# Writing the expert loop of the tensor engine's program out straight

## The chip, the core and the metric

One NeuronCore of a Trainium2 chip runs the whole step. The metric is the device time of one execution in microseconds (us); lower is better. Engines are named as in the profile: PE is the tensor engine (PEld its weight loads), DVE the vector engine, ACT the scalar engine, POOL GpSimd, SP the engine that issues nearly all of the transfers.

## The reference, cut to what matters

One layer of a hybrid decoder for 272 prompt and 8 sample rows (the 16 meta rows need no expert work, so 264 rows go on), all in float32. First a mixer (a Mamba-2 group and a convolution group), which the change does not touch. Then a mixture of experts:

```
logits = u @ w_router + b_router            # 32 experts, the top 4 of each row
gt  = min(x @ w_gate[e] + b_gate[e], 7)
up  = clip(x @ w_up[e] + b_up[e], -7, 7)
hdn = (up + 1) * gt * sigmoid(1.702 * gt)
y   = hdn @ w_down[e] + b_down[e]           # times the gate, added into the row
```

Each expert has three 1024 x 1024 float32 matrices, 12 MB, and all 32 experts are read from HBM: 192 pieces of 2 MB. How many rows an expert gets depends on the data and is known only on the chip.

## The kernel before, in words

The experts are sorted on the chip by their number of rows and paired: a round is one big expert (up to 128 rows) and one small expert (up to 32 rows). There are 16 rounds. The weights go through a ring in SBUF of six slots of 2 MB, `landed[0]` to `landed[5]` being the semaphores that tell of their landing: slots 0 and 1 hold w_gate, 2 and 3 w_up, 4 and 5 w_down. SP refills a slot with the next expert's weights as soon as PE tells that it has read it (lines 359 to 367, semaphores `gate_half`, `gate_used`, `piece_used`). So at most six transfers, one expert, are ahead of PE.

A big expert with 64 rows or fewer is narrow: every weight piece is read by PE once (`by_width(count, ...)` takes `what(1)`). One with more is wide: every piece is read twice, once for each half of its rows (`what(2)`). `by_width` (line 1546) builds both variants, so both stand in the program and the one that is not needed is jumped over. The order of PE in a round is: `big_expert` (line 1678): bias, gate pieces with the results of the former expert scattered between them, up pieces, inputs of the small expert gathered, hidden rows turned, down pieces; then `small_expert` (line 1712): gate pieces, with the scatter of the big expert between them (its shape goes by the big expert's width, `former`), up pieces, inputs of the next big expert gathered (its shape goes by `following`), turn, down pieces.

Products of a big expert are recorded at line 1482, of a small one at line 1525, bias products at 1472 and 1515, scatters at 1534 and 1492, gathers at 1503 and 1459, turns at 1228. The first bias of a round is the first group of line 1472 in it, so this line marks where rounds begin. One product in the source is two weight loads and two matmuls in the trace (16 source calls are a row "x32"); a turn is one of each.

Experts 0 and 1 (round 0) are written out ahead of the loop (lines 1738 and 1739). The other 15 rounds are one loop on PE (line 1740). Waits in it compare a semaphore with a register that is computed from the loop's counter, and the two widths that a round needs are read from the list `cnts` in SBUF (`count_of`, line 1553). ACT, DVE and SP run loops of their own, which stay.

Of the kernel before, what the change touches and what calls it, by code (L numbers as in the profile page):

```python
# [24 lines left out]
NE, TOPK = 32, 4  # L25
# [22 lines left out]
def build(nc, I, O):  # L48
    ctx = ExitStack()
    with ctx:  # L50
# [1172 lines left out]
        def _(pe):  # L1223
# [246 lines left out]
            def bias(bank, row):  # L1470
                for h_, dst in enumerate(halves(bank)):
                    MM(dst, oh[row:row + NE, :], brow[row:row + NE, 512 * h_:512 * (h_ + 1)],  # L1472
                       start=True, stop=False, skip_group_check=True)

            def piece_products(p, b, src, bank, fresh, i16):
                pe.wait_ge(landed[p // 2], i16)
                hs = []
                for k in range(2):
                    kk = 2 * (p % 4) + k
                    o = 512 * b + P * (kk % 4) + HALF * (kk // 4)  # L1480
                    for h_, dst in enumerate(halves(bank + b)):
                        hs.append(MM(dst, src[:, o:o + HALF], piece(p)[:, k, 512 * h_:512 * (h_ + 1)],  # L1482
                                     start=(fresh and kk == 0), stop=(kk == KT - 1), skip_group_check=True))
                return hs
# [44 lines left out]
            def scatter_s(m, n4, release=False):  # L1529
                if m:  # L1530
                    pe.wait_ge(ev["acc_done"], n4 + m)
                for h_ in range(2):
                    q = m // 2 + 2 * h_
                    h = MM(ps[:, 6 + h_, 0:TN], ys[QUAR * q:QUAR * (q + 1), P * (m % 2):P * (m % 2 + 1)],  # L1534
                           Pm[QUAR * q:QUAR * (q + 1), 0, :], start=True, stop=True)
                    if release and h_ == 0:
                        h.then_inc(ev["gate_used"], 1)
                h.then_inc(ev["sc_done"], 1)
# [14 lines left out]
            def count_of(i):  # L1553

                return pe.value_load(cnts[0:1, bass.ds(i, 1)], min_val=0, max_val=TN)
# [54 lines left out]
            def up_of(n, i16):  # L1610
                if n == 1:
                    for p in range(4, 8):
                        hs = piece_products(p, 0, xT, 2, False, i16)
                        hs[-1].then_inc(ev["up_first" if p == 7 else "piece_used"], 1)
                else:
                    bias(1, 64)
                    bias(3, 96)
                    for p in range(4):
                        hs = piece_products(p, 1, xT, 0, False, i16)
                        if p % 2:  # L1620
                            hs[-1].then_inc(ev[("gate_half", "gate_used")[p // 2]], 1)
                    for p in range(4, 8):
                        hs = piece_products(p, 0, xT, 2, False, i16)
                    hs[-1].then_inc(ev["up_first"], 1)
                    for p in range(4, 8):
                        hs = piece_products(p, 1, xT, 2, False, i16)
                        if p < 7:
                            hs[-1].then_inc(ev["piece_used"], 1)
# [45 lines left out]
            def former_ready(i):  # L1674
                pe.wait_ge(ev["p_ready"], i + 1)
                pe.wait_ge(ev["y_back"], i * 2 + 64)

            def big_expert(i, count, then=None):
                pe.wait_ge(ev["oh_ready"], i + 1)
                bias(0, 64)  # L1680
                if then:
                    then()
                pe.wait_ge(ev["xt_ready"], i * 2 + 2)
                bias(2, 96)

                def gate_up(n):
                    for p in range(4):
                        hs = piece_products(p, 0, xT, 0, False, i * 16 + 16)
                        if n == 1 and p == 1:
                            hs[-1].then_inc(ev["gate_half"], 1)  # L1690
                        if p == 3:
                            hs[-1].then_inc(ev["gate_done"], 1)
                        if p == (1 if then else 0):
                            former_ready(i)
                        for m in (() if then and p == 0 else (p - 1,) if then and p < 3 else (2, 3) if then else (p,)):
                            scatter_s(m, i * 4, n == 1 and m == 3)
                    if then:
                        pe.wait_ge(ev["order_ready"], 1)
                    up_of(n, i * 16 + 16)

                by_width(count, gate_up)
                pe.wait_ge(ev["s_ready"], i + 2)
                gather_s()
                by_width(count, lambda n: turn_hidden(n, i * 2))
                pe.wait_ge(ev["acc_done"], i * 4 + 4)
                pick_slots()
                pe.wait_ge(ev["xg_out"], i * 2 + 4)
                turn_s(xg, 2, ev["xt_done"])
                by_width(count, lambda n: down_of(n, i * 2, i * 16 + 16))
                pe.wait_ge(ev["ht_ready"], i * 2 + 2)  # L1710

            def small_expert(i, former, following):
                pe.wait_ge(ev["oh_ready"], i + 1)
                pe.wait_ge(ev["xt_ready"], i * 2 + 2)

                def former_rows(n, p):
                    if p == 0:
                        former_ready(i)
                    scatter(n, p, i * 4)

                by_width(former, lambda n: gate_s(i * 16 + 16, lambda p: former_rows(n, p)))
                up_s(i * 16 + 16)
                pe.wait_ge(ev["s_ready"], i + 2)
                by_width(following, gather)
                pe.wait_ge(ev["hdn_ready"], i * 2 + 2)
                turn_s(hdn, 0, ev["ht_done"])
                pe.wait_ge(ev["acc_done"], i * 4 + 4)
                pick_slots()

                def turn_following(n):  # L1730
                    for b in range(n):
                        pe.wait_ge(ev["xg_out"], i * 2 + 3 + b)
                    turn(n, xg, 2, ev["xt_done"])

                by_width(following, turn_following)
                down_s(i * 2, i * 16 + 16)

            big_expert(0, first, find_order)
            small_expert(1, first, count_of(3))
            with pe.Fori(0, NE // 2 - 1) as ii:  # L1740
                count, following = count_of(ii * 2 + 3), count_of(ii * 2 + 5)
                big_expert(ii * 2 + 2, count)
                small_expert(ii * 2 + 3, count, following)
            pe.wait_ge(ev["o_tab"], 1)
            n_over = pe.value_load(otab[0:1, OVER:OVER + 1], min_val=0, max_val=OVER)
            pe.wait_ge(ev["xt_ready"], NE * 2 + 2)
# [103 lines left out]
```

## Time and profile before

| | us |
|---|---|
| three runs | 1265.29, 1269.01, 1271.62 |
| median | 1269.01 |
| the profiled execution's own time | 1267.89 |
| its span, first to last instruction | 1266.1 |
| PE busy in the span | 1171.0 (92%) |
| DVE busy | 487.8 (39%) |
| mean granted PE clock | 0.974 of full speed |

Busy time of PE is modelled at its end and says little by itself. The mixer and the routing take the span up to about 300 us; experts run from there to about 1254 us; the rest is the final norm.

### The profile page before, as it was taken

How to read it: one execution, taken by the hardware profiler on the slowest of the kernel's cores; microseconds unless marked ns; L12 is line 12 of the kernel's file. 1: busy time of each engine (PE TensorE's matmuls, PEld its weight loads, DVE VectorE, ACT ScalarE, POOL GpSimd, SP SyncE). 2: the span in 40 equal slices, each digit the busy share in tenths (PEclk: the TensorE clock that was granted, in tenths of full speed). 3: DMA queues.
4: the chain of work that ended last, by engine and by line, in shares of the span. 5: the costliest groups of instructions: out<-in, count | busy, mean ns of one | idle time of the engine just before them, and what ended most of it. 6: DMA issues, size and time to landing. Idle time of an engine off the chain costs nothing.

```text
span 1266.1 us, 21176 instructions
## 1 busy us (share of the span) xinstructions
PE 1171.0 (92%) x8462; PEld 553.0 (44%) x8463; DVE 487.8 (39%) x1083; ACT 196.0 (15%) x432; POOL 5.4 (0%) x33
## 2 busy tenths in 40 slices
PE   8999989999899999999899999899999888979896
PEld 6888768874333333433333433333433333233233
DVE  2999997015332322232312233222232232323233
ACT  2144513021111111011101111100111111011012
POOL 0000000000000000000000000000000000000000
PEclk9999998999998999999989999999999899999898
DMA  9542338615999999899999999998999999999995
GB/s 394 226 170 88 121 148 313 272 44 193 396 428 424 429 427 424 338 430 429 429 428 386 358 430 429 429 429 353 396 430 429 429 429 427 430 429 428 428 431 215
DMA packets 36996, 451.35 MB, mean 357 GB/s; under 512 B 5112, under 2 KB 5656, under 8 KB 10080
## 3 DMA queue, kind: packets, MB, share of 16 engines
q1 hardware_dynamic: 35344, 449.02, 85.2%
q10 hardware_dynamic: 1616, 1.82, 0.4%
q8 instruction: 26, 0.43, 0.1%
q14 instruction: 10, 0.08, 0.0%
HBM read 443.57 MB, written 7.25 MB: 356 GB/s over the span
## 4 chain that ended last, share of the span: by engine, by line
PE 57%; DMA 28%; DVE 11%; issue 2%; DVEq 1%; ACT 0%; POOL 0%; SPq 0%; POOLq 0%; ACTq 0%
DMA ring<-in_w_experts 28%; PE ps L1482 23%; PE ps L1525 10%; DVE acts L734 5%; PE ps L1254 3%; PE ps L1459 3%; PE ps L1361 3%; PE ps L1418 2%; PE ps L1492 2%; PE ps L1534 2%; PE ps L1228 2%; PE ps L1472 1%; DVE acts L829 1%; PE ps L1352 1%; PE ps L1515 1%
## 5 line engine op out<-in xcount | busy, mean ns | idle before, releaser
L1482 PE MATMUL ps<-ring,extra 128*64 128x512 f32 x1824 | 418.4, 603 | 12.2 <-DMA ring<-in_w_experts 12.2
L1087 DVE TENSOR_TENSOR acts<-ps,acts 128x528 f32<-128x528 f32 x128 | 90.6, 708 | 393.1 <-PE ps L1492 199.5
L1525 PE MATMUL ps<-ring,extra 128*32 128x256 f32 x3072 | 207.2, 405 | 37.0 <-DMA ring<-in_w_experts 31.2
L1482 PEld LDWEIGHTS ps<-ring,extra 128*64 128x64 f32 x1824 | 123.0, 138 | 262.4 <-issue 233.5
L1525 PEld LDWEIGHTS ps<-ring,extra 128*32 128x32 f32 x3072 | 91.2, 114 | 142.6 <-issue 51.4
L734 DVE SCALAR_TENSOR_TENSOR acts<-acts,small 128x256 f32<-128x256 f32 x224 | 91.2, 474 | 1.1 <-ACT acts L461 1.1
L1254 PE MATMUL ps<-acts,ring 128*128 128x280 f32 (+1 forms) x320 | 75.3, 394 | 0.3 <-ACT ring L534 0.3
L1254 PEld LDWEIGHTS ps<-acts,ring 128*128 128x128 f32 x320 | 60.5, 190 | 14.2 <-issue 1.0
L1254 PE MATMUL ps<-acts,extra 128*128 128x280 f32 x256 | 61.3, 400 | 1.9 <-DVE acts L716 1.9
L1101 DVE TENSOR_SCALAR extra<-ps 128x512 f32<-128x512 f32 x32 | 22.0, 689 | 97.6 <-PE ps L1482 82.1
L1459 PE MATMUL ps<-acts 128*64 128x512 f32 (+1 forms) x228 | 57.3, 623 | 0.0
L614 ACT ACTIVATE extra<-extra 128x512 f32<-128x512 f32 x32 | 19.7, 630 | 235.8 <-DVE extra L1092 235.8
L1254 PEld LDWEIGHTS ps<-acts,extra 128*128 128x128 f32 x256 | 48.4, 190 | 14.2 <-issue 2.8
L1228 PE MATMUL ps<-small,extra 128*128 128x128 f32 x220 | 38.9, 290 | 13.5 <-DVE extra L1106 12.3
L1492 PE MATMUL ps<-acts,extra 64*128 64x264 f32 x304 | 51.1, 426 | 0.0
L1124 DVE SCALAR_TENSOR_TENSOR acts<-ps,acts 128x264 f32<-128x264 f32 x48 | 22.2, 490 | 64.8 <-ACT acts L644 64.7
L1534 PE MATMUL ps<-acts,extra 32*128 32x264 f32 x256 | 45.9, 434 | 0.8 <-DVE acts L1087 0.8
L1228 PEld LDWEIGHTS ps<-small,extra 128*128 128x128 f32 x220 | 22.9, 140 | 47.7 <-issue 21.0
L609 ACT ACTIVATE extra<-ps 128x512 f32<-128x512 f32 x34 | 20.4, 600 | 147.9 <-PE ps L1459 139.8
L1534 PEld LDWEIGHTS ps<-acts,extra 32*128 32x128 f32 x256 | 19.3, 184 | 53.1 <-issue 51.9
L1076 DVE TENSOR_SCALAR extra<-ps 128x256 f32<-128x256 f32 x16 | 6.8, 424 | 88.6 <-PE ps L1525 88.6
L624 ACT ACTIVATE extra<-ps 128x512 f32<-128x512 f32 x32 | 17.4, 594 | 129.4 <-PE ps L1482 129.4
(299 smaller groups left out, 895.9 us busy)
## 6 DMA issues: line engine op xcount, KB each, us to landing
ring<-in_w_experts SPq DMA_DIRECT2D x192, 2048.0 KB, 20.5
ring<-in_w_in_t SPq DMA_DIRECT2D x5, 2048.0 KB, 20.9
extra<-in_w_in_t SPq DMA_DIRECT2D x4, 2048.0 KB, 11.0
extra<-in_w_out_t SPq DMA_DIRECT2D x4, 1024.0 KB, 5.9
ring<-in_w_out_t SPq DMA_DIRECT2D x4, 1024.0 KB, 6.0
ring<-in_state_t SPq DMA_DIRECT2D x8, 512.0 KB, 7.4
ring<-dtx_rows SPq DMA_DIRECT2D x8, 512.0 KB, 6.4
out_ssm_s_t<-ring SPq DMA_DIRECT2D x8, 512.0 KB, 5.4
```

The costliest lines, as they stand in the source:

```text
L734: STT(conv[:, m, 0:SEQ], cbuf[:, m, k:k + SEQ], cw[:, m, k:k + 1], conv[:, m, 0:SEQ], ALU.mult, ALU.add).then_inc(ev["tap_added"], 1)
L1087: TT(both, ps[:, 6:8, 0:TN], both, ALU.add).then_inc(ev["acc_done"], 1)
L1124: return STT(Pm[:, bank, :], ps[:, 6, 0:TN], slot_id[:, slot:slot + 1], gp, ALU.is_equal, ALU.mult)
L1228: return nc.tensor.transpose(out, in_, ident[0:r, 0:r])
L1254: h = MM(ps[:, tile_bank(j), 0:T - lo], win(c)[:, k, P * q:P * (q + 1)], uT[:, k, lo:T], start=(k == 0), stop=(k == KT - 1))
L1361: h = MM(ps[:, m, 0:TN], wout(4 + k // 2)[:, k % 2, P * m:P * (m + 1)], conv[:, k, :], start=(k == 0), stop=False, skip_group_check=True)
L1418: h = MM(ps[:, m, 0:TN], wout(k // 2)[:, k % 2, P * m:P * (m + 1)], yT[:, k, :], start=False, stop=(k == KT - 1), skip_group_check=True)
L1459: h = MM(dst, S[0:r, j, HALF * b:HALF * (b + 1)], xn[0:r, j, 512 * h_:512 * (h_ + 1)], start=(j == 0), stop=(j == 2))
L1482: hs.append(MM(dst, src[:, o:o + HALF], piece(p)[:, k, 512 * h_:512 * (h_ + 1)], start=(fresh and kk == 0), stop=(kk == KT - 1), skip_grou ...
L1492: h = MM(ps[:, 6 + h_, 0:TN], ys[rows, 512 * b + P * m:512 * b + P * (m + 1)], Pm[rows, b, :], start=(b == 0), stop=(b == n - 1))
L1525: hs.append(MM(dst, src[:, o:o + QUAR], piece(p)[:, k, 256 * q:256 * (q + 1)], start=(fresh and kk == 0), stop=(kk == KT - 1), skip_group_ ...
L1534: h = MM(ps[:, 6 + h_, 0:TN], ys[QUAR * q:QUAR * (q + 1), P * (m % 2):P * (m % 2 + 1)], Pm[QUAR * q:QUAR * (q + 1), 0, :], start=True, sto ...
```

## The change

PE's loop over 15 rounds becomes a Python loop that writes 15 rounds one after the other. Every wait of it compares with a constant. The width of the following big expert is read once and handed on, where the loop read two a round. Products, their order, semaphores, the ring, and the programs of the other engines stay.

```diff
             big_expert(0, first, find_order)
             small_expert(1, first, count_of(3))
-            with pe.Fori(0, NE // 2 - 1) as ii:
-                count, following = count_of(ii * 2 + 3), count_of(ii * 2 + 5)
-                big_expert(ii * 2 + 2, count)
-                small_expert(ii * 2 + 3, count, following)
+            count = count_of(3)
+            for i in range(2, NE, 2):
+                following = count_of(i + 3)
+                big_expert(i, count)
+                small_expert(i + 1, count, following)
+                count = following
             pe.wait_ge(ev["o_tab"], 1)
```

## Rows read from the trace of the kernel before

**Rows 1.** The page: busy time of the engines; then transfers in 40 equal slices.
```profile
PE 1171.0 (92%) x8462; PEld 553.0 (44%) x8463; DVE 487.8 (39%) x1083; ACT 196.0 (15%) x432; POOL 5.4 (0%) x33
GB/s 394 226 170 88 121 148 313 272 44 193 396 428 424 429 427 424 338 430 429 429 428 386 358 430 429 429 429 353 396 430 429 429 429 427 430 429 428 428 431 215
ring<-in_w_experts SPq DMA_DIRECT2D x192, 2048.0 KB, 20.5
```

**Rows 2.** The chain that ended last, 358 to 727 us: start, us, what.
```profile
358.73 1.20 PE ps L1472 x8
...
369.98 7.04 PE ps L1482 x32
...
414.30 1.20 PE ps L1472 x8
...
468.30 1.23 PE ps L1472 x8
...
541.55 1.20 PE ps L1472 x8
...
652.57 1.20 PE ps L1472 x8
...
725.79 1.20 PE ps L1472 x8
```

**Rows 3.** Timeline of PE, 372 to 640 us: start, us, engine, line, [idle before <-releaser].
```profile
376.92 1.64 PE L1503 MATMUL ps<-acts 128*32 128x256 f32 x24
379.40 0.66 PE L1228 MATMUL ps<-small,extra 128*128 128x128 f32 x4 [0.84 <-DVE extra L1106]
...
452.27 1.07 PE L1525 MATMUL ps<-ring,extra 128*32 128x256 f32 x16
454.01 1.93 PE L1525 MATMUL ps<-ring,extra 128*32 128x256 f32 x32 [0.67 <-DMA ring<-in_w_experts]
...
468.30 1.23 PE L1472 MATMUL ps<-acts 32*64 32x512 f32 x8 [0.53 <-issue]
...
636.55 3.63 PE L1525 MATMUL ps<-ring,extra 128*32 128x256 f32 x32 [1.39 <-DMA ring<-in_w_experts]
```

**Rows 4.** Who PE waited for, 541.5 to 652.5 us: in total, times, longest.
```profile
PE ps L1525 <- DMA ring<-in_w_experts: 3.9, 3, 1.5
PE ps L1482 <- DMA ring<-in_w_experts: 1.4, 2, 1.0
```

**Rows 5.** Timeline of PE around its three longest waits for its own program.
```profile
323.52 1.64 PE L1503 MATMUL ps<-acts 128*32 128x256 f32 x24 [1.82 <-issue]
325.08 0.66 PE L1228 MATMUL ps<-small,extra 128*128 128x128 f32 x4
...
342.38 1.05 PE L1525 MATMUL ps<-ring,extra 128*32 128x256 f32 x10
346.37 3.83 PE L1525 MATMUL ps<-ring,extra 128*32 128x256 f32 x35 [2.94 <-issue]
...
398.59 1.92 PE L1525 MATMUL ps<-ring,extra 128*32 128x256 f32 x12 [2.84 <-issue]
```

**Rows 6.** DMA queues, windows 0:300, 300:358.7, 347:399, 358.7:414.3, 414.3:1266: packets, MB, share.
```profile
q8 instruction: 12, 0.20, 0.2%
...
q8 instruction: 5, 0.08, 0.5%
...
q8 instruction: 6, 0.10, 0.7%
...
q8 instruction: 7, 0.11, 0.8%
...
q8 instruction: 2, 0.03, 0.0%
```

**Rows 7.** Waits of PE for its own program, whole span; then 414.3:468.3.
```profile
PE ps L1472 <- issue: 8.0, 15, 0.6
...
PE ps L1472 <- issue: 1.1, 2, 0.5
```

**Rows 8.** The chain: round 0's groups beside the loop's of rows 2.
```profile
326.71 7.02 PE ps L1482 x32
358.43 0.29 issue
```
**Rows 9.** Stretches of 414.3 to 468.3 and 468.3 to 541.55 us: PE, PEld, DVE, ACT, POOL, clock, DMA share, GB/s.
```profile
414.30:468.30 54.00, 51.53 (x425) 18.83 (x425) 17.01 (x34) 6.62 (x14) 0.00 (x0) 1.00 1.01 428
468.30:541.55 73.25, 71.95 (x532) 26.92 (x533) 17.19 (x34) 6.76 (x14) 0.00 (x0) 1.00 0.94 388
```

## The prediction

> **What bounds the kernel now.** I read the page first [rows 1]. PE is busy 92% of the span, which suggests PE; the transfers say otherwise. From slice 11 to the end of the expert phase they stand at 424 to 431 GB/s, except in three places (338; 386 and 358; 353 and 396). The weights are 192 pieces of 2 MB; a round needs 12 of them, 25.2 MB, and at 430 GB/s that is 58.5 us. So I compared rounds with 58.5 us, by the chain of waits, where the first bias group (line 1472) marks the start of each [rows 2]. Round 1 lasts 414.30 - 358.73 = 55.6 us, of which 2.84 us is a stall that the loop's first pass alone has [rows 5], so a narrow round costs PE about 52.7 us. Round 3 is wide: 541.55 - 468.30 = 73.3 us, and there the transfers fall to 388 GB/s while PE is busy 71.95 of 73.25 us [rows 9]. Rounds 4 and 5 last 652.57 - 541.55 = 111.0 us together against 2 x 52.7 = 105.4: in them PE waits 3.9 + 1.4 = 5.3 us for weights [rows 4]. Then round 6 is wide again (725.79 - 652.57 = 73.2), and the pattern of three comes once more. After round 9 all rounds are narrow and go at the pace of the transfers.
>
> So the bound alternates. A microsecond lost by PE in a wide round, or just ahead of one, is a microsecond on the end, because the ring is full and the transfers stop. A microsecond lost in a narrow round costs nothing as long as a wait for weights follows that can swallow it: 0.67 us in round 2 [rows 3], 5.3 us in rounds 4 and 5 [rows 4] and as much in 7 and 8, about 5.8 us in each round from 10 on.
>
> **The change, part by part.**
>
> *The loop's edge and its reads.* The gap ahead of a round's first bias is 8.0 us over 15 rounds, 0.53 us each [rows 7]. Going from round 0 into the loop, which has two reads of widths but no jump back, it is 0.29 us [rows 8]. The straight program has one read and no jump, so I take 0.29 and save 0.25 a round. Bounds: 0 (if the gap is the read's latency), 0.53 (if it vanishes). It reaches the end only where PE binds: ahead of rounds 2, 3, 6 and 9, as the other gaps lie ahead of a wait for weights. 4 x 0.25 = -1.0 us; ends 0 and -2.1.
>
> *Waits on constants.* Round 0 is already written this way. Its 16 up calls take 7.02 us [rows 8], the loop's 7.04 [rows 2]; I take 0. PE's products hide the register work. If a tenth of a microsecond per wait came free it would show in this pair, so both ends are within 0.3 us.
>
> *PE's code must now be fetched.* This is the term that matters. Queue q8 carries instruction packets of 16 KB (0.11 MB in 7) [rows 6]. They come through the mixer (12 up to 300 us), in round 0 (5), in the first pass over the loop (7), and then none until the 2 for the epilogue: the 14 later passes run from what PE holds. So q8 is the queue of PE's program. Counting the source, both widths included, the body has 370 products of four instructions, 28 turns of two and some 57 waits, reads and branches: 1,590, or 1,560 without the register work. Each straight round therefore brings 6 to 7 packets of its own.
>
> What a fetch costs PE can be read at three places, all of them in code met for the first time [rows 5]: 1.82 us after the up products of expert 0, 2.94 us in expert 1 after ten products past the first up bias, 2.84 us in expert 3, four products into up. Every one follows a jump over an unused wide variant. The last two are 1,537 instructions apart by my count, with 6 packets between them [rows 6]: 256 instructions a packet. Where nothing is jumped over, PE spends about 55.6/6.5 = 8.5 us on a packet and the next one arrives unseen. The stall comes where a jump leaves little of a packet to execute. The one bad place is the small expert's gate-to-up jump, over 52 calls (some 210 instructions).
>
> A straight round is 1,563 instructions, 27 more than six packets, so the packet border moves back by 27 instructions against the code from round to round. From the three stalls I take 6 us from the moment that a packet is asked for until it can be used, and get at this jump, for rounds 1, 2, 4, 5, 7, 8: 3.2, 3.0, 2.2, 1.2, 0.3, 1.4 us. In wide rounds the code jumped over is the short variant and the rest runs slower, so I expect next to nothing at this jump; at the start of a wide round, a jump over the narrow gate and up (163 instructions) comes close behind the down products, at 1.0 us in round 3 and 0.5 in round 9. The jump after the big expert's up products costs little even when it stalls: in round 0, 325.08 - 321.69 = 3.4 us lie between the up products' end and the turn, in round 1 379.40 - 377.02 = 2.4, since the turn waits for DVE anyway [rows 2, 3, 5]; 1.0 us.
>
> On the path: round 1 has its 2.84 us now, so +0.4. Round 2: +3.0, less the 0.67 us wait at 454.01 that follows it [rows 3]: +2.3. Rounds 4 and 5: 3.4 us against 5.3 us of waits, of which 1.39 comes after round 5's jump [rows 3, 4]: 0. Rounds 7 and 8: 0. Wide rounds: +1.5. Rounds 10 to 15: each has about 5.8 us to spare: 0. Sum +4.2 us. The ends: 0 if every fetch is covered, and the case that each round stalls like rounds 0 and 1 (below).
>
> *The fetches take transfer time.* 14 passes x 6.1 packets = 86 packets, 1.4 MB, 3.3 us at 430 GB/s. About 500 of the 900 us are at the transfers' pace: +1.8 us; ends 0 and 3.3. That holds if the packets are spread over the 16 DMA engines. Were all to go through one, that engine would do 6 more packets a round beside the 96 that it has now for 12 pieces: 3.6 us a round. Against it: in the first pass, with 7 packets in 55.6 us, the round was no longer than PE's own work and its stall.
>
> *A rule weighed.* The row says: no q8 packet and a gap of 0.53 us at the loop's edge. The Trainium skill ("Runtime: NRT & Kernel Launch", section "Instruction fetch mechanics") says that instruction memory is a first-in first-out buffer, that a taken branch whose target is outside a window of two pages forces a fetch, and that kernels therefore prefer full unrolling. By that rule the jump back over six pages should pay a fetch each round and the change should remove it. The trace disagrees for PE: 14 jumps back, no packet. The same section gives PE 128 KiB and 256 instructions a block, which would hold this body, and with that the trace agrees.
>
> Sum: -1.0 + 0 + 4.2 + 1.8 = +5.0 us on the profiled execution's 1267.9 us (span 1266.1 and 1.8 outside): **1272.9 us**. The median of the three runs, 1269.01, is 1.1 us above the profiled one, well inside their spread, so I do not shift it.
>
> **The rivals.**
>
> *A. Every round stalls as at first sight* (slower). Rounds 0 and 1 have three stalls, 7.6 us, or 3.8 us a round. With that, rounds 1 to 9 gain 9 x 3.8 - 2.8 = 31.4 us of stall; the waits that swallow it are 0.67 + 5.3 + 5.3 = 11.3; less 1.0 for the edges, plus 1.8: +21 us, 1289 us. It decides from the point where two narrow rounds stall for more than 5.3 us together. For: these are the only samples of unseen code between wide products. Against: two of the three sit at the same packet phase by accident of 1,537 being near six packets, and the phase drifts.
>
> *B. The loop's edge is dearer than it looks* (faster). If each jump back hides a fetch like that of the page's rule, 2.9 us a round, four of them on the path go: 1267.9 - 11.6 = 1256 us. Against: the gap is 0.53 us and q8 is silent [rows 6, 7].
>
> *C. All fetches are covered.* Then only the edges and the transfer time remain: 1267.9 - 1.0 + 1.8 = 1268.7 us. For: 12 packets in the mixer left no stall of this kind. Against: the mixer has no jumps.
>
> **How the numbers follow.** My forecast has 0.60, A 0.20, B 0.04, C 0.16. Within 0.5% is within 6.3 us of the runs' median, about what a measurement of this kernel tells from no change. My forecast's own range is 1267 to 1281, of which a third lies beyond 1275.4; A lies beyond it nearly always; C hardly. Slower: 0.60 x 0.27 + 0.20 x 0.85 = 0.33; faster: B and a little noise, 0.05; same 0.62. The range goes from 1265.5 to 1286, into A.
>
> **What would show it.** q8 with about 86 more packets (some 112 in all), spread evenly from 414 us on. Issue waits of PE at line 1525, 1 to 3 us long, in the small experts of the early rounds, weaker towards round 7, then back after round 8. The gap ahead of line 1472 at 0.3 us or less. Rates in the wide rounds' slices a little lower, elsewhere 429 or 428. Groups of 16 calls still at 7.0 us. I am wrong if q8 stays silent, if stalls of 2 to 3 us come in every narrow round (A), if the narrow rounds after round 9 get longer than 59 us, or if a wide round loses more than 3 us.

## The result, and the profile after

| | before | after |
|---|---|---|
| median of the runs timed side by side, us | 1268.79 (4 runs, 1265.29 to 1271.62) | 1287.36 (4 runs, 1280.46 to 1291.35) |
| ratio, 95% interval | | 1.014 (1.0108 to 1.0171) |
| the profiled execution, us | 1267.89 | 1291.35 |
| its span, us | 1266.1 | 1289.5 |
| mean granted PE clock | 0.974 | 0.960 |

The straight program is slower by 18.6 us, 1.4%. The profiled execution is the slowest of its four, 4.0 us above their median, so the sums below explain 23.4 us of span and are a little larger than the typical loss.

The page of the kernel after, lines that answer to [rows 1] and [rows 6]:

```profile
PE 1187.9 (92%) x8462; PEld 559.4 (43%) x8462; DVE 488.4 (38%) x1083; ACT 196.0 (15%) x432; POOL 5.4 (0%) x33
GB/s 395 221 159 125 80 149 309 278 66 188 397 426 426 427 425 381 309 428 425 428 424 357 373 427 425 425 423 322 393 426 426 424 427 425 426 426 426 427 425 170
q8 instruction: 111, 1.82, 0.6%
```

PE executes the same matmuls in 16.9 us more (1187.9 against 1171.0), and its mean granted clock is lower, 0.960 against 0.974. The transfers' rate in the ten slices ahead of the last is 424 to 427 GB/s where it was 427 to 431. The program's packets went from 26 to 111, evenly: 6 a round, 5 to 8 at the extremes.

Where PE waited in the expert rounds, kernel after, then kernel before (in total, times, longest, us):

```profile
PE ps L1525 <- DMA ring<-in_w_experts: 20.6, 17, 2.3
PE ps L1482 <- DMA ring<-in_w_experts: 13.3, 9, 2.9
PE ps L1525 <- issue: 13.1, 5, 3.3
PE ps L1503 <- issue: 9.8, 5, 2.6
...
PE ps L1515 <- issue: 6.5, 2, 3.9
...
PE ps L1482 <- issue: 1.2, 1, 1.2
PE ps L1459 <- issue: 0.4, 1, 0.4
```
```profile
PE ps L1525 <- DMA ring<-in_w_experts: 31.2, 23, 2.3
PE ps L1482 <- DMA ring<-in_w_experts: 12.2, 13, 1.2
...
PE ps L1525 <- issue: 2.8, 1, 2.8
```

Two things changed hands. The 8.0 us ahead of line 1472 [rows 7] are gone altogether. In their place stand 31.0 us of waits for the program, at lines 1525, 1503, 1515, 1482 and 1459, nearly all shortly behind a jump over an unused variant. The waits for weights shrank by 9.5 us: that much was swallowed.

Rounds, from first bias to first bias, in us (the last runs to the end of the span):

| round | 1 | 2 | 3 | 4 | 5 | 6 | 7 | 8 | 9 | 10 | 11 | 12 | 13 | 14 | 15 |
|---|---|---|---|---|---|---|---|---|---|---|---|---|---|---|---|
| before | 55.6 | 54.0 | 73.3 | 49.3 | 61.7 | 73.2 | 49.3 | 61.7 | 73.2 | 49.4 | 58.1 | 58.7 | 58.7 | 58.7 | 72.4 |
| after | 54.6 | 59.1 | 75.4 | 50.6 | 64.1 | 72.5 | 50.5 | 65.7 | 72.5 | 53.4 | 60.6 | 58.0 | 57.9 | 59.7 | 74.4 |
| late at the round's end | 0.8 | 5.9 | 8.0 | 9.3 | 11.7 | 11.0 | 12.2 | 16.1 | 15.4 | 19.4 | 21.9 | 21.2 | 20.3 | 21.3 | 23.4 |

So the 23.4 us fall into three parts. 1.7 us are lost before round 1 begins (360.44 against 358.73 us), in code that the change doesn't touch: over all profiled executions of this document, round 1 begins between 351.8 and 360.4 us. 13.7 us are lost in rounds 1 to 9, and 8.0 us in the six narrow rounds behind them.

Stretches of the kernel after, rounds 2, 3 and 5, against [rows 9] (PE, PEld, DVE, ACT, POOL, clock, DMA share, GB/s):

```profile
415.10:474.20 59.10, 54.80 (x432) 19.82 (x428) 17.00 (x34) 6.62 (x14) 0.00 (x0) 0.94 1.01 426
474.20:549.60 75.40, 73.43 (x540) 27.03 (x536) 17.20 (x34) 6.76 (x14) 0.00 (x0) 0.98 0.89 357
...
600.20:664.30 64.10, 55.80 (x430) 19.57 (x427) 17.02 (x34) 6.61 (x14) 0.00 (x0) 0.92 1.01 427
```

Round 2 lost 5.1 us: 1.8 in idle time (59.10 - 54.80 = 4.3 against 54.00 - 51.53 = 2.5) and 3.3 in work done at a lower clock (54.80 against 51.53, clock 0.94 against 1.00). The place, in the timeline of PE (kernel after; start, us, [idle before]) and in short stretches of it:

```profile
453.81 0.64 PE L1525 MATMUL ps<-ring,extra 128*32 128x256 f32 x8 [0.67 <-DMA ring<-in_w_experts]
456.73 0.64 PE L1525 MATMUL ps<-ring,extra 128*32 128x256 f32 x8 [2.28 <-issue]
457.30 0.63 PE L1515 MATMUL ps<-acts 32*32 32x256 f32 x8
457.86 4.48 PE L1525 MATMUL ps<-ring,extra 128*32 128x256 f32 x48
```
```profile
454.00:457.00 3.00, 0.72 (x16) 0.16 (x8) 0.98 (x4) 0.42 (x1) 0.00 (x0) 1.00 0.98 410
457.00:460.00 3.00, 3.00 (x40) 1.26 (x36) 0.00 (x0) 0.00 (x0) 0.00 (x0) 0.67 0.99 421
460.00:464.00 4.00, 4.00 (x40) 1.50 (x32) 1.27 (x3) 0.00 (x0) 0.00 (x0) 0.82 1.04 438
```

PE waits 0.67 us for weights, runs eight matmuls, waits 2.28 us for its program, and then the granted clock falls from 1.00 to 0.67 and 0.82 in the stretches behind: the lower of its two levels (1.2 GHz) for part of each. Before, the same place had only the 0.67 us wait [rows 3] and the clock stayed at 1.00. This wait for the program is paid twice: as idle time, and in the work behind it.

The end of the transfers, kernel after, then kernel before (same columns):

```profile
1264.00:1266.00 2.00, 2.00 (x24) 0.99 (x20) 0.00 (x0) 0.00 (x0) 0.00 (x0) 0.50 0.58 246
1268.00:1270.00 2.00, 2.00 (x11) 0.36 (x7) 0.61 (x2) 0.00 (x0) 0.00 (x0) 1.00 0.47 197
1270.00:1272.00 2.00, 2.00 (x26) 1.10 (x28) 0.23 (x1) 1.65 (x4) 0.00 (x0) 1.00 0.27 107
```
```profile
1246.00:1248.00 2.00, 2.00 (x18) 0.82 (x14) 0.00 (x0) 1.35 (x4) 0.00 (x0) 1.00 0.71 303
1248.00:1250.00 2.00, 2.00 (x38) 1.02 (x40) 1.68 (x4) 1.57 (x3) 0.00 (x0) 1.00 0.12 49
```

Before, all 16 DMA engines finish together: 303 GB/s in one stretch, 49 in the next. After, the stream peters out: 246, 197 and 107 GB/s over some eight microseconds, because some engines are behind the others. Each of the 16 engines reports its own share of a piece. For the last piece, after the first report, in us:

```
before  0.05 0.08 0.09 0.11 0.14 0.18 0.23 0.26 0.32 0.33 0.35 0.60 1.81 1.88 1.93
after   0.15 0.19 0.44 0.58 1.56 1.57 1.82 6.35 7.63 7.79 8.02 8.02 8.16 9.48 9.51
```

PE can start a piece when the last of the 16 reports is in. Before, that is 1.9 us behind the first, after 9.5 us, with eight engines 6 to 9.5 us behind. I call this the spread. In a wide round the transfers stop and it falls back; from round 10 on nothing resets it, and it grows over the tail as 3.4, 4.9, 6.4, 8.0, 9.5 us. About 30 code packets between 946 and 1239 us raised the sum of the engines' lags by 49 us, some 1.6 us a packet, where the packets' own records last 1.0 to 1.1 us and one of weights takes 0.61 us.

The reports also split the loss. In round 10 the first report of a piece comes 16.0 us later than before, and for the last piece 15.8 us: the foremost engines lost nothing more in the tail. The last report of the last piece is 23.4 us later, 15.8 and 7.6 of added spread. As PE was 15.4 us late at the start of round 10, the spread is 7.6 of the 8.0 us that the tail lost, and the 20 us that PE waited for its code in rounds 10 to 13 cost next to nothing.

### The profile page after: what moved, and what is told of

It is laid out like the page before. It is cut to its first block, busy times and chain, and to the rows that moved or that the text cites. A ratio compares the mean times of both kernels' runs of the same rounds, so it can differ in the third digit from the quotient of the medians.

```text
span 1289.5 us, 20742 instructions
## 1 busy us (share of the span) xinstructions
PE 1187.9 (92%) x8462; PEld 559.4 (43%) x8462; DVE 488.4 (38%) x1083; ACT 196.0 (15%) x432; POOL 5.4 (0%) x33
## 4 chain that ended last, share of the span: by engine, by line
PE 64%; DMA 21%; DVE 11%; issue 3%; DVEq 1%; ACT 0%; POOL 0%; SPq 0%; POOLq 0%; ACTq 0%
PE ps L1482 26%; DMA ring<-in_w_experts 20%; PE ps L1525 11%; DVE acts L734 5%; PE ps L1459 3%; PE ps L1254 3%; PE ps L1534 3%; PE ps L1361 3%; PE ps L1492 2%; PE ps L1228 2%; PE ps L1418 2%; PE ps L1352 1%; PE ps L1472 1%; DVE acts L829 1%; PE ps L1515 1%
## 5 line engine op out<-in xcount | busy, mean ns | idle before, releaser
L1482 PE MATMUL ps<-ring,extra 128*64 128x512 f32 x1824 | 426.6, 614 | 14.5 <-DMA ring<-in_w_experts 13.3
L1525 PE MATMUL ps<-ring,extra 128*32 128x256 f32 x3072 | 211.6, 412 | 36.1 <-DMA ring<-in_w_experts 20.6
L1534 PEld LDWEIGHTS ps<-acts,extra 32*128 32x128 f32 x256 | 19.5, 186 | 53.8 <-issue 52.6
```

The source lines that it names most:

```text
L1525: hs.append(MM(dst, src[:, o:o + QUAR], piece(p)[:, k, 256 * q:256 * (q + 1)], start=(fresh and kk == 0), stop=(kk == KT - 1), skip_group_ ...
```

## The experiments

My theory after the result: PE's code is no longer resident, and this costs in two ways, by PE's waits for code (and the clock behind them) while PE binds, and by code packets that leave single DMA engines behind while the transfers bind. The rival is that only one of the two counts. The kernels were timed beside the kernel before, whose median was 1267.96 to 1270.44.

| kernel | median, us (range, runs) | ratio to before (95%) | q8 packets |
|---|---|---|---|
| tail_straight | 1277.77 (1275.30 to 1281.80, 7) | 1.0067 (1.0043 to 1.0091) | 63 |
| head_straight | 1280.02 (1273.71 to 1282.91, 7) | 1.0082 (1.0051 to 1.0113) | 81 |
| known_widths | 1272.51 (1267.61 to 1278.13, 10) | 1.0020 (0.9996 to 1.0045) | 71 |
| pe_delay | 1269.15 (1264.08 to 1274.65, 10) | 1.0001 (0.9978 to 1.0024) | 27 |
| spare_one | 1339.39 (1338.50 to 1356.92, 5) | 1.0577 (1.0529 to 1.0625) | 26 |
| spare_all | 1274.34 (1268.11 to 1279.85, 10) | 1.0043 (1.0013 to 1.0073) | 26 |
| loop_of_three | 1301.09 (1300.40 to 1306.66, 4) | 1.0277 (1.0228 to 1.0327) | 122 |
| straight_again | 1283.94 (1279.86 to 1285.80, 4) | 1.0120 (1.0074 to 1.0165) | 111 |
| tail_narrow | 1275.25 (1266.79 to 1279.02, 8) | 1.0043 (1.0016 to 1.0071) | 46 |
| pe_delay_long | 1453.58 (1450.55 to 1462.56, 6) | 1.1466 (1.1431 to 1.1501) | 153 |
| pe_idle | 1277.68 (1270.70 to 1286.02, and one of 3980.16, 7; without that one 1277.03) | 1.0072 (1.0046 to 1.0099) | 26 |
| head_known | 1268.75 (1264.24 to 1274.30, 10) | 0.9991 (0.9972 to 1.0010) | 58 |
| loop_padded | 1497.36 (1494.08 to 1503.25, 4) | 1.1810 (1.1760 to 1.1860) | 153 |

**Half of the rounds straight.** Rounds 1 to 9 or rounds 10 to 15 stay a loop.

```diff
 # tail_straight; head_straight the other way round: range(2, 20, 2), then pe.Fori(0, 6)
-            with pe.Fori(0, NE // 2 - 1) as ii:
+            with pe.Fori(0, 9) as ii:
                 ...
+            count = count_of(21)
+            for i in range(20, NE, 2):
+                following = count_of(i + 3)
+                ...
```

> Rounds 1 to 9 are the loop, rounds 10 to 15 written out straight. Late-landing theory: each 16 KB packet of PE's code holds its DMA engine back by about 1.5 us of weight transfer, all on part of the engines, and nothing takes that back until the transfers stop; the six straight rounds bring about 37 packets, so the last weights land about 8 us later and the time is 8 us longer (about 1277), with PE's waits for its own code mostly swallowed. Stall theory (what counts is PE waiting for its code ahead of a wide round): rounds 10 to 15 have about 6 us each to spare, so the time stays within 2 us of before.

> Rounds 1 to 9 straight, rounds 10 to 15 the loop (its first pass fetches, then q8 is silent). Late-landing theory: the first three rounds cost 6 us by PE's own waits, the two stretches up to the wide rounds 6 and 9 about 3.5 us each by late landings, the tail about 2 us for the one pass that fetches: +13 to +15 us, about 1283. Stall theory: nearly the whole loss of the straight program, +18 us or more, about 1287, as all three wide rounds are in this part.

tail_straight lost 9.8 us, head_straight 12.1; together 21.9, the change 18.6. The late-landing theory had 8 and 13 to 15, the stall theory up to 2 and 18 or more: the first is near in both, the second in neither. The profiled execution of head_straight is one of its fast ones, 6.1 us under its median. In the tail PE's waits for code are small beside those for weights. Waits of PE in tail_straight, 910 to 1260 us:

```profile
PE ps L1525 <- DMA ring<-in_w_experts: 27.6, 18, 3.1
PE ps L1482 <- DMA ring<-in_w_experts: 11.6, 7, 2.0
...
PE ps L1503 <- issue: 1.5, 2, 0.8
PE ps L1525 <- issue: 1.4, 1, 1.4
```

There are 2.9 us of waits for code against 39 us for weights that could swallow them, and the rounds still last 60.2, 60.2, 58.7, 60.3 us. The spread at the end is 9.6 us here too (1.9 before): 7.7 us of added lateness, in an execution whose span is 8.2 us longer than before (1274.2 against 1266.1). This shows the tail's loss nearly without PE's waits.

**Fewer packets in the tail.** tail_narrow is tail_straight with rounds 10 to 15 written for narrow experts only, so the unused variants are neither stored nor jumped over. Its program holds for these inputs alone, as do those of known_widths and head_known.

```diff
             def by_width(count, what):
+                if isinstance(count, str):
+                    what(1)
+                    return
 ...
+            for i in range(20, NE, 2):
+                big_expert(i, "narrow")
+                small_expert(i + 1, "narrow", "narrow")
```

> Rounds 1 to 9 are the loop; rounds 10 to 15 are straight and have only the narrow variant in the program, which is the one that these inputs take; for other inputs it would be wrong. About 3.3 packets a round against 6.2 in tail_straight, and no jump, so PE never waits for its code there. Late-landing theory: half the packets, about 20, on some 9 engines at 1.5 us each: the last weights land 3 to 4.5 us later than before, time +3 to +5 us against before (tail_straight +8.5). Stall theory: PE has no stall left, the time is that of before or 1 us less.

About 20 more packets in all instead of 37, a spread of 5.1 us instead of 9.6, and a loss of 6.0 us instead of 9.8. The intervals of the two losses overlap, so the medians alone don't show the difference. The traces do, where the tail is taken by itself, from the start of round 10 to the end of the span (us; "more" is against the kernel before, 356.1 us, 2 packets, spread 1.9):

| kernel | q8 packets in the tail | PE's waits for code | tail takes more | spread more |
|---|---|---|---|---|
| the change | 39 | 20.0 | 8.0 | 7.6 |
| the change once more | 39 | 17.6 | 8.5 | 7.7 |
| tail_straight | 39 | 2.9 | 7.9 | 7.7 |
| tail_narrow | 22 | 0 | 4.1 | 3.2 |
| known_widths | 22 | 0 | 4.5 | 3.5 |

The tail's loss follows the packets and the spread, and not PE's waits. An estimate from these rows: some 0.2 us a packet.

**Traffic on one DMA engine, and the same traffic on all.** The loop of before, with 96 more copies of 16.4 KB issued by ACT, six a round: each as a block that one engine carries (spare_one), or one that all 16 share (spare_all).

```diff
+            def spare(k):
+                a.dma_start(spare_d[k], expert_w[0, 0, 0:17, 0:241]).then_inc(ev["spare_in"], 16)
+            # spare_all: expert_w[0, 0, 0:1, :]
             def pair(big, small_):
+                spare(0)
                 sigmoid(big * 2)
                 ...
             with a.Fori(0, NE // 2 - 1) as ii:
                 output_out_s(ii * 2 + 1)
+                a.wait_ge(ev["spare_in"], ii * 96 + 96)
```

> The loop as before; ACT issues six spare copies of 16.4 KB a round (17 rows of 964 bytes, HBM to HBM, 96 in all), each meant to fall on one DMA engine as a packet of PE's code does; PE's program is untouched. Late-landing theory: they hold back the engine that they fall on. If always the same one, it loses up to 1.5 us for each copy, some 9 us a round, and the time grows by 80 to 130 us; if spread over several engines as the code packets are, +12 to +16 us. Rival (the packets cost only their own bytes, 1.6 MB in all): +2 to +4 us.

> The same with six spare copies of one row of 16 KB a round, which may be split over the 16 engines as 1 KB each. Theory that a foreign packet costs an engine a fixed time (about 0.9 us beside its own bytes): every engine loses it six times a round, +50 to +80 us. Theory that the cost goes by bytes: 1.5 MB more, +2 to +4 us, and no engine falls behind the others. If the row goes to one engine, this is spare_one over again.

The same 1.6 MB costs 70 us on one engine and 5.3 us on all. Both times miss what I expected (80 to 130 us; 2 to 4 us). PE's waits for code are nearly those of before in both. But the 70 us are not the price of late weights: the last line of the diff makes ACT wait in each round until the six copies of the round before have landed. Waits in spare_one, of PE (350 to 1300 us), then of ACT:

```profile
PE ps L1240 <- DVE extra L1118: 72.7, 14, 15.9
PE ps L1537 <- DMA ring<-in_w_experts: 19.3, 11, 4.2
PE ps L1494 <- DMA ring<-in_w_experts: 13.6, 11, 2.1
```
```profile
ACT extra L615 <- DMA spare<-in_w_experts: 377.9, 14, 36.4
```

ACT waits for its own copies, the hidden rows come late, and PE waits for them at the turn: 73.6 us in the whole span against 12.3 before and 12.2 in spare_all. PE's waits for weights are 35.3 us, less than the 43.4 before. Without that added wait some of the loss might have come by late weights instead; no run here separates the two. What spare_one does show is the lag itself: from 398 to 491 us the spread grew from 4.9 to 10.5 us with eight copies, some 0.7 us a copy, about what a copy's own packets take (17 of 45 ns). In the course of the run it reached 20.2 us. One engine alone is behind there; in the changed kernel eight are.

**Waits of PE against work of PE.** pe_delay adds five products (40 matmuls) ahead of the small expert's up products, where the code waits are. pe_delay_long adds twelve. pe_idle adds a wait for GpSimd at the same place, about as long as pe_delay's work.

```diff
                     if p == 4:
+                        pe.wait_ge(landed[2], i16)
+                    for _ in range(again if p == 4 else 0):      # 5; pe_delay_long: 12
+                        for q, dst in enumerate(quarters(2)):
+                            MM(dst, xT[:, 0:QUAR], piece(4)[:, 0, 256 * q:256 * (q + 1)], start=True, stop=False, ...)
# pe_idle
+                    pe.wait_ge(ev["idle_done"], rounds + 1)      # in small_expert, ahead of up_s
+            for r in range(1, NE // 2):                          # GpSimd
+                g.wait_ge(ev["gate_done"], 2 * r + 2)
+                ... 12 short memsets, the last tells idle_done
```

> The loop as before, but in its small experts the first four products of the up piece are issued five more times (into the same bank with start set, so the result is unchanged), about 1.25 to 2.5 us of PE work at the place where the straight program waits for its code; no packet is added. Bookkeeping of the prediction (PE's lost time is swallowed by the next waits for weights: 0.67 us in round 2, 5.3 us in each later stretch of three, all of it in rounds 10 to 15): with 1.25 us a round +3 us, with 2.5 us a round +9 us, about 1272 to 1278. Rival (each lost microsecond of PE counts): +19 to +37 us.

> As pe_delay, with the first products of the small experts' up piece issued twelve more times instead of five: about 5.3 us of PE work more in each round (five gave 2.2 us, and no change in the time), no packet added. More than the straight program's waits for code, which are 0.6 to 6 us a round, 28 us in all. Bookkeeping of waits for weights: rounds 1 to 3 lose 5 to 10 us, each later stretch of three 16 less 5.3 us; about +25 us, rounds 10 to 15 nearly free. If the time stays within 8 us of before, PE's own waits can't explain the straight program's loss at all.

> The loop as before, but ahead of each small expert's up pieces PE waits for a chain of 12 small GpSimd operations that starts when the gate products end: an idle wait of 2 to 4 us a round, where the straight program waits for its code, and where pe_delay worked on. No packet is added. It keeps whatever an idle wait does to the granted clock. Late-landing theory: like pe_delay, within 4 us of before. Rival (an idle PE loses clock after it, and that is what the straight program pays for): +8 to +20 us, with a mean clock at 0.95 to 0.96 as in the straight program.

Of pe_delay's 2.2 us of work a round (15 rounds, 33 us) nothing reaches the end: 1269.15. Its wide rounds are longer (75.4, 77.0 and 75.4 us against 73.3, 73.2 and 73.2), and rounds 5, 8 and 11, where PE has fewer waits for weights, give it back (57.0, 56.2 and 52.6 us against 61.7, 61.7 and 58.1). Its waits for weights fall to 23 us from 43.4. My own accounting had put 3 to 9 us on the end for a delay of this size; it had not counted round 11. pe_idle takes 7.8 us more (median of six, without the execution named below) for 37.1 us of idle time, and its interval lies wholly above pe_delay's. Its waits:

```profile
PE ps L1532 <- POOL idle_t L433: 37.1, 15, 2.8
PE ps L1479 <- issue: 8.0, 15, 0.6
PE ps L1532 <- DMA ring<-in_w_experts: 7.2, 7, 1.6
```

It has no packet more than before, and gives back in the same rounds (57.6, 55.9, 52.1 us), but the wide rounds last 77.0, 80.5 and 77.0 us, and narrow ones are longer too (round 7: 55.2 us against 51.5 in pe_delay). Round 6, pe_delay first, then pe_idle:

```profile
653.20:730.20 77.00, 75.70 (x574) 28.50 (x574) 17.19 (x34) 6.76 (x14) 0.00 (x0) 0.98 0.91 376
```
```profile
662.80:743.30 80.50, 76.93 (x532) 28.08 (x533) 17.19 (x34) 6.76 (x14) 1.49 (x12) 0.94 0.89 362
```

pe_idle's 532 matmuls are busy for longer than pe_delay's 574, at a clock of 0.94 against 0.98. The profiled execution of pe_idle lies 9.0 us over the median of the six, so its rounds overstate the loss. The medians over the executions say the same: a mean clock of 0.970 in pe_idle, 0.974 before beside it, 0.985 in pe_delay. So idle time and work of nearly the same length at one place are not the same: the second is free here, the first costs clock. Not after every wait: in round 2 of pe_idle the stretch behind the 2.52 us wait kept 1.00. One further execution of pe_idle took 3980.16 us; I cannot explain it. By the late-landing theory I had expected at most 4 us from pe_idle, and it missed; the rival had +8 to +20.

pe_delay_long missed too, for another reason. I expected some 25 us and measured 184. Its twelve products of 16 instructions make PE's loop body 1,785 instructions by my count instead of 1,593 (pe_delay: 1,673), and now the whole body is fetched again in each pass: 153 packets, with 93.0 us of waits ahead of line 1472, 6.2 to 7.1 us at each jump back.

**What is held, and what is not.** loop_of_three puts three rounds into the body, five passes. loop_padded adds to the body of one round 195 instructions that are never executed.

```diff
# loop_of_three
-            with pe.Fori(0, NE // 2 - 1) as ii:
+            with pe.Fori(0, 5) as ii:
+                for r in (0, 2, 4):
+                    count, following = count_of(ii * 6 + r + 3), count_of(ii * 6 + r + 5)
+                    ...
# loop_padded, at the end of the loop of before
+                with pe.If(count < 1):
+                    for _ in range(24):
+                        bias(0, 64)
```

> PE's loop has three rounds in its body and runs five times; 4,800 instructions, some 19 packets. If PE holds about eight packets (the one-round body, seven, stays resident), this body does not fit, all of it is fetched on each pass, and the time is that of the straight program, 1283 to 1292, with about 110 q8 packets. Rival (PE keeps more than it was seen to): q8 is silent after the first pass and the time is within 5 us of before.

> The one-round loop with 195 instructions more in its body that are never executed (products under a condition that these inputs never meet). pe_delay_long had a body of about the same size, 1,785 instructions, nine packets a round and a jump back of 6.5 us, but also 5.3 us more work in each round, and took 1453 us. If the size of the body alone makes PE fetch it again on each pass, q8 shows about 9 packets a round and the time is 1330 us or more. Rival (the work did it, and the packets are harmless): within 10 us of before.

Timeline of PE in loop_padded, the start of two passes and a jump between them:

```profile
581.54 2.10 PE L1472 MATMUL ps<-acts 32*64 32x512 f32 x8 [10.57 <-issue]
625.85 1.92 PE L1525 MATMUL ps<-ring,extra 128*32 128x256 f32 x12 [4.98 <-issue]
653.15 2.10 PE L1472 MATMUL ps<-acts 32*64 32x512 f32 x8 [10.97 <-issue]
```

and its page (the queue; then a group, with its busy time, mean ns | idle before):

```profile
q8 instruction: 153, 2.51, 0.7%
...
L1472 PE MATMUL ps<-acts 32*64 32x512 f32 x152 | 36.0, 958 | 150.5 <-issue 150.5
```

Nothing was added to what PE executes, and the time rises by 227 us, 150.5 of them ahead of the round's first bias. Its other waits for code stand mostly behind the jump to the small expert's up products, 3.7 to 5.4 us each. The bias products themselves take 958 ns each against 612 before and 614 in the changed kernel, and the mean clock of the span is 0.887. In loop_of_three the jump back costs 7.16, 7.3, 7.92 and 6.55 us where it can be seen in full:

```profile
548.47 2.10 PE L1472 MATMUL ps<-acts 32*64 32x512 f32 x8 [7.16 <-issue]
```

loop_of_three missed its forecast of 1283 to 1292 us, which had no price for these jumps: four of them are 28.9 us.

So a jump back outside what PE holds costs 6.2 to 11.9 us (the most in loop_padded, where a jump over the 195 unused instructions comes right ahead of it); one inside costs 0.53 us [rows 7]. The packets are more than the body, too. 1,785 instructions are seven packets by my count, and 9 came in a pass; three rounds are 18.7, and 21 came. An estimate from both is two packets for each jump back. That jump is rival B's mechanism, real but absent in the kernel before, whose body fits. The Trainium skill ("Runtime: NRT & Kernel Launch", section "Instruction fetch mechanics") ties the forced fetch to the jump's distance; these two kernels agree, while the loop of before jumps back 1,593 instructions with no packet, and its conclusion that unrolling is to be preferred fails here. The prediction took the 128 KiB of that section as room enough for the body; at 256 instructions to 16 KB that room would hold 1,785 as well, and these were not held.

**Straight code without jumps.** known_widths is the straight program with each width written in, head_known the same for rounds 1 to 9 with the tail's loop kept.

```diff
+WIDE = (6, 12, 18)
                 if isinstance(count, str):
+                    what(2 if count == "wide" else 1)
+                    return
             for i in range(2, NE, 2):                            # head_known: range(2, 20, 2)
-                following = count_of(i + 3)
-                big_expert(i, count)
+                big_expert(i, width(i))
                 ...
```

> All rounds straight and only the width that these inputs take is in the program for experts 1 to 31 (rounds 3, 6 and 9 wide), so nothing is jumped over; for other inputs it would be wrong. About 3.4 packets of code a round in place of 6.1 and no jump. Stall theory: PE never waits for its code; the three first stalls go too; the time is that of before or up to 5 us below it, 1264 to 1269. Late-landing theory: half the packets are left, about 20 in the last six rounds, so the last weights still land 2 to 4 us later, and each of the two stretches ahead of rounds 6 and 9 loses 1 to 2 us; less the 4 us of first stalls: 1268 to 1273.

> Rounds 1 to 9 straight with only the widths that these inputs take (3.4 packets a round, no jumps), rounds 10 to 15 the loop; for other inputs it would be wrong. Against head_straight (+10.4 us, 6.1 packets, jumps): what PE's waits for its code and the clock after them cost in rounds 1 to 9 goes away, and half the packets. If the head's loss is mostly late landings, half of it stays: +5 us. If it is mostly PE's waits, 0 to +2 us.

Waits of PE for its program in the rounds written straight, head_straight (360 to 975 us), then head_known (400 to 910 us):

```profile
PE ps L1515 <- issue: 5.3, 2, 3.0
PE ps L1503 <- issue: 5.2, 3, 2.1
PE ps L1525 <- issue: 5.0, 2, 4.3
...
PE ps L1459 <- issue: 1.2, 1, 1.2
PE ps L1472 <- issue: 1.0, 2, 0.6
PE ps L1482 <- issue: 0.9, 1, 0.9
```
```profile
PE ps L1472 <- issue: 0.3, 1, 0.3
```

head_known still fetches (58 packets), yet its waits for code are gone and so is the loss: 0.9991. head_straight loses 12.1 us. known_widths, straight to the end with 71 packets and no wait for code at all, comes to +4.5 us on the medians, with an interval that still holds 1; its spread at the end is 5.4 us, close to tail_narrow's 5.1 us. In the head it is therefore mostly the waits behind jumps that cost, not the packets. The split isn't clean: head_known also sheds the stalls of round 1 that the kernel before has [rows 5], and 23 of head_straight's packets. Nor is the head as steady as the tail. Rounds 1 to 9, from the start of round 1 to that of round 10, took 551.3 us in the profiled execution before. More than that, in us: 13.7 in the change, 11.1 in the change once more, 6.5 in head_straight, all with the same code there; 3.3 in known_widths and 0.8 in head_known, without waits for code; 0.5 in tail_straight and 3.7 in tail_narrow, where these rounds are the untouched loop. So without the waits the head is within what unchanged rounds show, and with them it is above.

**The change once more** (straight_again):

> The changed kernel once more, for its spread between executions. Late-landing theory: the time follows the number of packets that fall on the unluckiest DMA engine, so executions differ by steps of about 1.5 us; median 1283 to 1291. Stall theory: executions agree as closely as those of before.

1283.94 us, 14.9 above the kernel before beside it; the waits came at the same places with other lengths (round 2: 3.29 us instead of 2.28, round 3: 0.6 instead of 1.24), and the spread at the end was 9.7 us. Its four executions lie 5.9 us apart, those of the kernel before beside it 13.9 us, so the scatter favours neither theory.

No version is faster than the kernel before by more than its measurement is uncertain; head_known, the nearest, isn't a program for other inputs.

## Why the prediction was wrong, step by step

**What bounds the kernel: right.** Alternating bound, wide rounds by PE, the tail by the transfers. One reading in it was off: a narrow round costs PE 49.3 us at full clock (rounds 4 and 7), not 52.7, and round 10 (49.4 us) has no wait for weights, so it had no 5.8 us to spare of its own; rounds 11 to 15 had 5.4 to 7.2.

**The loop's edge: right in kind, half in size.** I took 0.25 us a round; all 0.53 us went, with no idle time left ahead of line 1472. It was my outer bound (-2.1 us on the path instead of -1.0).

**Waits on constants: right.** Sixteen up calls take 7.09 us in round 1 (7.04 before [rows 2]).

**The amount of code: right.** I forecast 86 more packets, 112 in all; there were 111.

**The first failed step: the price of PE's waits on the path, "Sum +4.2 us".** Where the waits come was right in the early rounds; what they cost was not. At the jump from gate to up of the small expert I expected 3.2, 3.0, 2.2, 1.2, 0.3 and 1.4 us in rounds 1, 2, 4, 5, 7 and 8. Measured there: 2.6, 2.3, 1.2, 0, 0 and 0 us. The wide round 3 began with 1.24 us (forecast 1.0). The fall towards round 7 is what the drift of the packet border gave. But two things were missing. I had written that the jump behind the big expert's up products costs little even when it stalls, and the 1.0 us that I named for it went into no sum; it held PE for 2.0 us in round 1, 1.25 in round 8 and 1.9 to 2.6 in rounds 10 to 12. And I priced a wait by its idle time only. Round 2 has a wait of 2.28 us and is 5.1 us longer, 3.3 of them work at a lower clock. And rounds 4 to 9, for which I had forecast next to nothing, took 7.4 us more. My +4.2 us stand against +13.7 for rounds 1 to 9 in the profile, +11.1 in the second one (on the medians head_straight +12.1, head_known -1.7). This is the larger part of the miss.

**"Rounds 10 to 15: each has about 5.8 us to spare: 0": right for PE's waits, wrong for the sum.** In rounds 10 to 13 there were 20 us of waits for code, more than anywhere. Rounds 10 and 11 lost 4.0 and 2.5 us, and rounds 12 and 13, with 8.5 us of such waits, gained 1.5. tail_straight, with 2.9 us of them, lost as much in the tail, and the first reports of the pieces came no later in the course of the tail; so its 8.0 us belong to the next step.

**The second failed step: "The fetches take transfer time: +1.8 us".** I priced the packets at their bytes, 3.3 us at 430 GB/s, spread over 16 engines, and bounded the case of one engine away with the first pass over the loop, which showed no loss. That pass is one in which PE binds; it could not show it. The spread could have: in the kernel before it stands at 3.5 us in round 2, behind the twelve packets of rounds 0 and 1, and at 1.6 to 2.0 us from round 4 on, outside the wide rounds. Measured, a packet holds its engine back some 1.6 us instead of 0.6, eight of the sixteen engines end up far behind, and the lag stays until the transfers stop, so that the last of 16 landings is 9.5 us behind the first instead of 1.9. The term is about +8 us in the tail alone (the added lateness of the last piece is 9.5 - 1.9 = 7.6; tail_straight as a whole +9.8), in a part of the kernel where I had put nothing at risk. The table of tails shows this cause; spare_one, with ACT's wait in it, doesn't.

**The rivals.** A (1289 us) came nearest to the time, but not by its mechanism: it wanted 3.8 us of stall in each of rounds 1 to 9, 34 us, and there were 11.0 us, while its price for the tail was nothing. That the sum came near 1289 is luck. B was excluded rightly for this loop and exists in longer ones. C's view that the fetches are covered fails by 31 us of waits. Of my marks for being wrong, one came true: rounds longer than 59 us behind round 9 (60.6 in round 11; 59.7 in 14). Wide round 3 lost 2.1 us, short of the 3 us that I had named.

**What stays open.** How the head's loss divides between idle time, clock and late landings (the spread at the entries of rounds 6 and 9 was 4.9 and 5.1 us, against 1.8 and 1.6 before) is not settled; head_known and known_widths only show that it goes when the waits go. Why a code packet costs its engine 1.6 us when its record lasts 1.07, why eight engines, and what uneven traffic costs by late weights alone, without ACT's wait, no run here tells.

## What to carry to other kernels

A loop body that an engine holds costs nothing to repeat, so before writing a loop out straight, or adding to its body, count its instructions and look whether the program's queue is silent in the later passes: here 1,593 and 1,673 were held, 1,785 were not, and the step cost 15 to 18%. When transfers are the bound, don't price small extra transfers by their bytes alone: find which DMA engines they fall on, since a piece has landed only when the slowest engine is through, and a lag persists as long as the stream doesn't stop. Price a wait of PE in a busy stretch with the clock that follows it, not with its idle time alone; work in its place can be free.

## What the runs showed of the hardware that I had not expected

- Capacity is all or nothing. With 1,673 instructions in the body (by my count) a pass fetches none; with about 1,785, seven packets, it fetches 9 each pass, and the jump back takes 6.2 to 11.9 us.
- A code packet of 16 KB delays its DMA engine by some 1.6 us in a saturated stream (49 us of lag over 30 packets), against 0.61 us for a weight packet of the same size. A copy of that size that carries data puts its engine some 0.7 us behind.
- Code fetches are uneven: eight of sixteen engines lay 6 to 9.5 us behind at the end. With 39 code packets in the last six rounds these took 7.9 to 8.5 us more, with 22 packets 4.1 to 4.5.
- Idle waits of about 2.5 us, one a round, cost 7.8 us, with the mean clock at 0.970 (median of six executions); 2.2 us of work at that place cost nothing measurable, with the clock at 0.985.
